# PEER query weights multiplied as fp32 without a split, nine chunks of them loaded into idle memory, and a new order of ring slots

## The reference

```python
h = rms_norm(x, norm2_g[l]) * (1 + scale2) + shift2
q = (h @ w_q).reshape(B, S, 8, 2, 128)              # w_q: 1024 x 2048
sk = einsum('bshpd,hpnd->bshpn', q, sub_keys)       # 8 heads, 2 halves, 128 keys
top_s, top_i = top_k(sk, 16)                        # per half
best_s, best_pos = top_k(all 256 sums of a head, 16)
gates = softmax(best_s)
act = gelu(einsum('tkd,td->tk', u[idx], h))         # 128 experts per token
y = einsum('tk,tkd->td', gates * act, v[idx])
x = x + gate2 * y
```

## Time and profile before

| | |
|---|---|
| time, median of 3 runs | 1796.01 us (1795.46 to 1796.23) |
| the profiled execution | 1796.63 us |
| its span | 1794.8 us |
| busy share PE / DVE / ACT / POOL | 83% / 74% / 32% / 28% |
| bytes moved | 663.24 MB, mean 370 GB/s |

### The profile page before, as it was taken

The page is one execution under the profiler, slowest core; times in us unless marked ns, Lnnn a source line. Parts: engine busy times, 40 slices in busy tenths (PEclk is TensorE's granted clock), DMA queues, the critical chain, the costliest instruction groups (busy, mean ns, idle before and its releaser), DMA issues.

```text
span 1794.8 us, 17891 instructions
## 1 busy us (share of the span) xinstructions
PE 1485.2 (83%) x6040; PEld 886.1 (49%) x6040; DVE 1330.4 (74%) x3039; ACT 577.5 (32%) x1285; POOL 510.6 (28%) x556
## 2 busy tenths in 40 slices
PE   3999999877778787777799999997777778887787
PEld 2999896333233333333378998853333333333333
DVE  7898898776776777675579886986777676777554
ACT  3565542221222222221245664331222222221222
POOL 0000014433334343334200000243333333433430
PEclk8999999989989999999999999999898988989999
DMA  9877879999999999999967754999999999999995
GB/s 382 275 263 261 293 300 400 421 421 421 422 421 422 421 421 421 422 421 421 421 222 261 255 194 131 370 421 421 421 422 421 421 422 421 421 422 421 422 421 221
DMA packets 102619, 663.24 MB, mean 370 GB/s; under 512 B 11776, under 2 KB 11904, under 8 KB 31488
## 3 DMA queue, kind: packets, MB, share of 16 engines
q0 software_dynamic: 79488, 578.85, 78.6%
q1 hardware_dynamic: 23040, 83.26, 13.2%
HBM read 661.01 MB, written 1.05 MB: 369 GB/s over the span
## 4 chain that ended last, share of the span: by engine, by line
DMA 45%; PE 36%; DVE 13%; ACT 2%; issue 2%; SPq 1%; POOL 0%; DVEq 0%; ACTq 0%
DMA big<-pairs,big 24%; DMA late<-pairs,big 21%; PE yac L707 15%; PE acc L448 10%; PE pg L448 5%; DVE big L1259 2%; DVE wsp L427 1%; DVE late L1259 1%; DVE big L1079 1%; PE acc L601 1%; DVE big L1145 1%; PE acc L574 1%; DVE big L1144 1%; ACT big L895 1%; DMA big<-ada 1%
## 5 line engine op out<-in xcount | busy, mean ns | idle before, releaser
L707 PE MATMUL yac<-big 128*128 128x512 f32 x1216 | 605.2, 646 | 190.0 <-ACT big L895 190.0
L707 PEld LDWEIGHTS yac<-big 128*128 128x128 f32 x1216 | 240.7, 204 | 533.8 <-issue 273.9
L1464 POOL DMA_INDIRECT big<-pairs,big x304 | 289.6, 953 | 599.1 <-PE yac L707 492.3
L707 PE MATMUL yac<-late,big 128*128 128x512 f32 x832 | 401.0, 624 | 58.0 <-ACT big L895 58.0
L707 PEld LDWEIGHTS yac<-late,big 128*128 128x128 f32 x832 | 164.0, 201 | 285.0 <-issue 198.1
L1464 POOL DMA_INDIRECT late<-pairs,big x208 | 199.4, 959 | 275.9 <-PE yac L707 248.1
L1259 DVE CUSTOM_DVE_ANT_0 big<-big,acc 128x1024 f32<-128x1024 f32 x148 | 179.9, 1220 | 113.4 <-DMA big<-pairs,big 113.1
L448 PE MATMUL acc<-hs,wsp 128*128 128x256 f32 x2016 | 260.1, 287 | 3.6 <-DVE wsp L427 3.6
L886 ACT ACTIVATE big<-big 128x4 f32<-128x4 f32 (+1 forms) x138 | 28.3, 205 | 709.6 <-DVE big L1259 709.6
L448 PEld LDWEIGHTS acc<-hs,wsp 128*128 128x128 f32 x2016 | 247.3, 192 | 10.7 <-issue 9.9
L1259 DVE CUSTOM_DVE_ANT_0 big<-big,pg 128x1024 f32<-128x1024 f32 x156 | 187.4, 1219 | 78.0 <-DMA big<-pairs,big 77.5
(11 more groups left out here) (137 smaller groups left out, 1018.6 us busy)
## 6 DMA issues: line engine op xcount, KB each, us to landing
raw<-stream SPq DMA_DIRECT2D x132, 512.0 KB, 4.5
big<-ada_pairs POOLq DMA_DIRECT2D x40, 1024.0 KB, 7.2
big<-ada SPq DMA_DIRECT2D x16, 512.0 KB, 13.7
big<-pairs,big POOLq DMA_INDIRECT x304, 21.5
late<-pairs,big POOLq DMA_INDIRECT x208, 22.0
big<-subkeys SPq DMA_DIRECT2D x2, 1024.0 KB, 13.6
x<-xT SPq DMA_DIRECT2D x1, 1024.0 KB, 10.1
con<-consts SPq DMA_DIRECT2D x1, 706.0 KB, 4.6
```

What stands on the lines that cost most here:

```text
L707: mm = pe.matmul(yac[:, 2 * t + w, :], diag(n), row(L, n)[:, D + w * 512:D + (w + 1) * 512], start=(n % (SLOTS // TT) == 0), stop=(n % (SL ...
L1464: g.indirect_dma_start(row(L, n), None, pairs, bass.IndirectOffsetOnAxis(ap=col(Q_IDX + n).bitcast(U32), axis=0)).then_inc(row_in[SLOT_OF[ ...
```

## The change

1. The query weights are no longer split. PE multiplies the raw fp32 chunk with the fp32 source in `big` (B_H): one fp32 matmul of 256 columns per 128 rows in place of three fp32r ones. The 16 `act_high` and 16 `dve_low` of these chunks go, the low part of the source goes too. `h2_by_tokens` has 8 transposes in place of 16 matmuls.
2. Chunks 4 to 12 are *parked*: nine loads go straight to idle pieces of `big` (in places 0, 1, 6, 7 of the ring and half of 5), issued by SP once the last output product is done. Chunks 0 to 3 and 13 to 15 still go through the raw buffers, which come free when their product is done (`wq_done`).
3. Chunks 0 and 1 are first made for tokens 0 to 127 alone (`query_first`), so that head 0's scores of that half come out early; their other half follows.
4. The `late` places are free at once. The picks' places begin with `FIRST`: 8 to 13, 2, 3, 0, 1, 6, 7, twice. Places 0, 1, 6, 7 wait for the parked chunks in them: for chunks 5, 7, 9 and 11 to be multiplied. Places 4 and 5 hold the source and wait for the second `h2_by_tokens`.
5. DVE runs heads 0 and 1 of the search without a break, then groups 0 to 3 of the dots with head 2 between them. Four groups of `add_pick`, not two, stand among the chunks, behind 7, 9, 11 and 13.

```diff
+LOWS = 3
-TOPK_WQ = ((1, 0, 0), (1, 0, 1), (1, 0, 2), (2, 0, 3), (4, 1, 0), (4, 1, 1), (5, 1, 2), (6, 1, 3),
-           (9, 2, 0), (9, 2, 1), (11, 2, 2), (11, 2, 3))
-DOTS_WQ = (8, 10)
-GATES_WQ = (9, 11)
-GELU_WQ = (9, 11)
-DIAG_WQ = (10, 12)
-PICKS_WQ = (11, 13)
-EXP_WQ = 6
+H2TOK_WQ = 3
+EXP_WQ = 4
+GELU_WQ = (6, 8, 10, 12)
+PICKS_WQ = (7, 9, 11, 13)
-CYCLE = [0, 1, 2, 3, 8, 9, 4, 5, 6, 7, 10, 11, 12, 13]
+FIRST = [8, 9, 10, 11, 12, 13, 2, 3, 0, 1, 6, 7]
+CYCLE = FIRST[:2] + [4, 5] + FIRST[2:]
+BRIDGE = CYCLE[:12] + FIRST[:2] + CYCLE[12:]
+LAST_CYCLE = BRIDGE[2:]
+SLOT_OF = (FIRST * 2 + CYCLE * 8 + BRIDGE + LAST_CYCLE * 8)[:SLOTS]
+PARK_AT = (0, CH, ROW, ROW + CH, 6 * ROW, 6 * ROW + CH, 7 * ROW, 7 * ROW + CH, 6 * ROW - CH)
+M_PARK = M_WQ + 4
...
+                    if n == M_PARK:
+                        chunk_used(sp, L, M_OUT + N_OUT - 1)
+                        for j in range(PARKED):
+                            load_parked(L, j)
...
+            def query(L, c, out, t0, t1):
+                for k in range(KD):
+                    mm = pe.matmul(out, chunk_raw(L, M_WQ + c)[:, k * P:(k + 1) * P], col(B_H + k * T + t0, t1 - t0),
+                                   start=(k == 0), stop=(k == KD - 1))
+                return mm
...
+            def query_first(L):
+                pe.wait_ge(acc_free, nth(L, EVACS, E_WQ + 2))
+                for c in range(2):
+                    raw_landed(pe, L, M_WQ + c)
+                for k in range(KD):
+                    pe.wait_ge(src_hi, nth(L, 4 * KD, 3 * KD + k + 1))
+                    for c in range(2):
+                        mm = pe.matmul(acc[:, (E_WQ + c) % 2, 0:P], chunk_raw(L, M_WQ + c)[:, k * P:(k + 1) * P],
+                                       col(B_H + k * T, P), start=(k == 0), stop=(k == KD - 1))
+                mm.then_inc(q0_done, 1)
+                pe.wait_ge(q0_taken, L + 1)
+                pe.wait_ge(subkeys_in, nth(L, 16, 16))
+                for p in range(2):
+                    mm = pe.matmul(yac[:, 2, p * P:(p + 1) * P], col(B_QP + p * T, P), col(B_SUB + p * P, P),
+                                   start=True, stop=True)
+                mm.then_inc(sk0_done, 1)
+                for c in range(2):
+                    query(L, c, acc[:, (E_WQ + c) % 2, P:T], P, T).then_inc(wq_done, 1)
...
-                first_two(L, M_WQ, E_WQ, 3)
-                head_subkeys(L, 0)
+                query_first(L)
                 for c in range(2, N_WQ):
-                    by_features(L, M_WQ + c, E_WQ + c)
-                    if c >= 4 and c % 2 == 0:
+                    query_chunk(L, c)
+                    if c == 2:
+                        head_subkeys(L, 0)
+                    elif c == 3:
+                        head_subkeys(L, 1)
+                    elif c >= 6 and c % 2 == 0:
                         head_subkeys(L, c // 2 - 1)
...
-                source(L, 3, 1)
-                for c in range(N_WQ):
...
+                normalised(nth(L, 2, 2), gs[:, KD:2 * KD])
+                for n in range(len(ADA_WQ)):
+                    ada_next(L, ADA_OUT + N_OUT + n)
+                for u in range(2):
+                    scores_in(L, u)
+                    for part in range(4):
+                        topk_part(L, u, part)
+                unit_gates(L, 0)
+                for g in range(len(GELU_WQ)):
+                    pick_dots(L, g)
+                    pick_weights(L, g)
+                    if g < 2:
+                        if g == 0:
+                            scores_in(L, 2)
+                        topk_part(L, 2, 2 * g)
+                        topk_part(L, 2, 2 * g + 1)
...
                     before = USES[r].index(n) - 1
                     if before >= 0:
                         pool.wait_ge(slot_done, L * SLOTS + USES[r][before] + 1)
-                    elif RING_BIG <= r < RING_BIG + W:
-                        pool.wait_ge(chunk_done, (L + 1) * SPLITS + r - RING_BIG + 1)
-                    elif r >= RING_BIG + W:
+                    elif r >= RING_BIG:
+                        pool.wait_ge(chunk_done, (L + 1) * SPLITS + min(r - RING_BIG + 1, W))
+                    elif r in (4, 5):
                         pool.wait_ge(h2tok_done, L * TT + TT)
+                    else:
+                        inside = [j for j, at in enumerate(PARK_AT) if at // ROW == r]
+                        if inside:
+                            pool.wait_ge(wq_done, nth(L, N_WQ, M_PARK - M_WQ + inside[-1] + 1))
```

More of the change, by code:

```diff
@@ L286, in build @@
         index_done = sem("index_done")
+        parked_in = [sem(f"parked_in{j}") for j in range(PARKED)]
+        wq_done = sem("wq_done")
+        q0_done = sem("q0_done")
+        q0_taken = sem("q0_taken")
+        sk0_done = sem("sk0_done")
+        sk0_taken = sem("sk0_taken")
         row_in = [sem(f"row_in{r}") for r in range(RING)]
@@ L445, in product @@
                 if source is not None:
-                    pe.wait_ge(src_done, nth(L, 4 * KD, source * KD + k + 1))
+                    pe.wait_ge(src_done, nth(L, LOWS * KD, source * KD + k + 1))
                 for n, (a, b) in enumerate(TERMS):
@@ L461, in _, with load, load_next, load_parked @@
             sp.dma_start(cact, cB).then_inc(c_in, 16)
[L463 to L471, removed]
+            def load(L, m):
+                n = streamed(L, m)
+                sp.dma_start(raw[:, n % RAW, :], stream[nth(L, CHUNKS, m), :, :]).then_inc(landed[n % RAW], 16)
+            def load_next(L, m):
+                before = m - RAW
+                if before < M_PARK + PARKED <= m:
+                    before -= PARKED
+                if before < SPLITS:
+                    sp.wait_ge(split_done, nth(L, SPLITS, before + 1))
+                else:
+                    sp.wait_ge(wq_done, nth(L, N_WQ, before - M_WQ + 1))
+                load(L, m)
+            def load_parked(L, j):
+                sp.dma_start(col(PARK_AT[j], CH), stream[nth(L, CHUNKS, M_PARK + j), :, :]).then_inc(parked_in[j], 16)
             def load_first(k):
@@ L494, in _ @@
             for L in range(depth):
-                for n in range(RAW, SPLITS):
+                for n in range(RAW, CHUNKS):
+                    if n == M_PARK:
+                        chunk_used(sp, L, M_OUT + N_OUT - 1)
+                        for j in range(PARKED):
+                            load_parked(L, j)
+                    if parked(n):
+                        continue
                     load_next(L, n)
@@ L678, in h2_by_tokens @@
                 for k in range(KD):
[L679 to L683, removed]
+                    mm = pe.transpose(out[:, k // 4, k % 4 * P:(k % 4 + 1) * P], col(B_H + k * T + t * P, P), ident)
                 mm.then_inc(h2tok_done, 1)
             def head_subkeys(L, h):
-                if h == 0:
-                    pe.wait_ge(subkeys_in, nth(L, 16, 16))
                 pe.wait_ge(acc_free, nth(L, EVACS, E_WQ + 2 * h + 1 + 3))
@@ L694, in head_subkeys @@
                 out = yac[:, 2 + h % 2, :]
-                for t in range(TT):
+                for t in range(0 if h else 1, TT):
                     for p in range(2):
@@ L812, in modulated @@
                     act.wait_ge(xn_done, nth(L, 2 * KD, w * KD + k + 1))
-                    nc_act.activation(hs[:, 0, k * T:(k + 1) * T], col(B_H + k * T, T), ACT.Identity,
+                    out = col(B_H + k * T, T) if w else hs[:, 0, k * T:(k + 1) * T]
+                    nc_act.activation(out, col(B_H + k * T, T), ACT.Identity,
                                       bias=mod[:, 24 * w + k:24 * w + k + 1]).then_inc(src_hi, 1)
@@ L977, in _ @@
                 a.clear()
-                for c in range(N_WQ):
[L979 to L983, removed]
+                query_first_store(L)
+                for c in range(2, N_WQ):
+                    query_store(L, c)
+                    if c == 2:
                         store_subkeys(L, 0)
-                    if c >= 4 and c % 2 == 0:
+                    elif c == 3:
+                        store_subkeys(L, 1)
+                    elif c >= 6 and c % 2 == 0:
                         store_subkeys(L, c // 2 - 1)
```

122 lines of the change are left out of this document (70 added, 52 removed).

## The result

The changed kernel takes 1824.72 us (median of 4 runs, 1824.24 to 1825.77), the one before in the same session 1796.12 (1795.46 to 1796.34). The ratio is 1.0162, with a 95% interval of 1.0148 to 1.0175: 28.6 us slower, where 23 were forecast (1819 us, range 1803 to 1831). The profiled execution has a span of 1823.9 us, 29.1 more than before.

What follows compares the result with a forecast made beforehand. The prediction took the DMA stream at 421 GB/s as the bound, so time lost before each plateau counts. Layer 0 +10.9, layer 1 +9.6 and slower PE starts +2.8 made +23 us: 1819 us, range 1803 to 1831.

Steps and rivals of the forecast that it cites:

- The measure: Before each layer's DMA plateau: lost transfer time, length x (1 - rate/421), each microsecond lost being one of the end.
- Part 1, the products: PE's query products: an fp32 chunk takes 3.41 us, 0.5 more than a split one.
- Part 2, the first indices: Head 0's search in layer 0: begins at 229.0, first gather issued near 236.0, 3.8 us earlier.
- Parts 3 and 4, the order and the waits: PE's chunks and POOL's in-order waits, layer 0: pick 10 goes at 272.0 behind chunk 9, pick 11 at 286.5 behind chunk 11.
- Part 5, the ledger: DMA losses before the plateau: 29.1 us against 18.2 in layer 0, 40.2 against 30.6 in layer 1.
- The two big holes: DMA gaps ahead of picks 10 and 11: 7.7 and 12.0 us in layer 0, 10.9 and 12.0 in layer 1.
- The first row: From the output stage to the full DMA queue: 7.7 us lost in layer 0, 14.3 in layer 1.
- the second starvation: Behind the second transposes PE waits for head 1's dots; pick 30's bytes flow just when the queue runs dry, loss put at 0.
- rival C: Starvation behind the second transposes costs 3 to 6 us per layer: 1825 to 1831 us and more; chance 13%.
- the slower PE behind a stand: PE's start on group 2 of the picks after standing some 8 us: 1.4 us per layer, +2.8 in all.
- Rival A: DMA queue stays fed, no hole before picks 10, 11 and 26: 1769 us, milder form near 1777; chance 11%.
- Rival B: No change: chunk near 2.8 us or PE about 5 us per pair of chunks faster, 1793 to 1799 us; chance 6%.

Runs made afterwards that it cites:

- e4: Changed kernel with another order of places: places 6 and 7, which wait for chunks 9 and 11, come only at picks 18 and 19; 1808.79 us, ratio 1.0054.
- e10: e9 with the four groups of picks one chunk later, behind chunks 8, 10, 12 and 14; 1787.61 us, ratio 0.9946.
- e8: Changed kernel with six of the eight 128-row pieces in every query product; 1807.46 us, ratio 1.0060.
- e5: e1 plus the edit of e3 and a new order of places, with places 4 and 5 at picks 28 and 29; 1792.18 us, ratio 0.9965.
- e1: Changed kernel with nothing parked, all 16 query chunks going through the four raw buffers; 1803.35 us, ratio 1.0030.
- e2: e1, but gathers into places 0, 1, 6 and 7 still wait for chunks 5, 7, 9 and 11; 1827.92 us, ratio 1.0169.
- e7: Changed kernel with two groups of picks among the query chunks, behind 11 and 13, in place of four; 1813.97 us, ratio 1.0096.
- e11: e5 without the edit of e3, so head 1's exponential stays behind the last query copies; 1805.94 us, ratio 1.0053.
- e3: Changed kernel with the exponential of head 1's picks moved to behind ACT's copy of chunk 14; 1820.01 us, ratio 1.0124.
- e9: e5 with chunks 4 to 7 parked again in places 0 and 1, which come last in the round, at picks 10 and 11; 1791.57 us, ratio 0.9973.

## Why the prediction was right

**The measure.** Transfer time lost before the plateau, per layer, was the right currency. The eleven kernels that followed came out within 3 us of their expectations by the medians; against the kernel before of their own session e4 and e10 gained some 4 us more than expected. Each was worked out with the traces so far at hand, so they bear the account out, and not the first forecast.

**Part 1, the products.** 3.41 us forecast, 3.46 measured. That they don't cost one for one is shown by e8 (0.6 of a microsecond for each) and by e5, which has the same products and is faster than the kernel before. That they cost by way of the waits is what e8's gathers 10 and 11 suggest, 5.6 and 7.4 us earlier.

**Part 2, the first indices.** 236.0 forecast, 237.4 measured, in a run whose output stage ended 0.5 us later. The slower start was as charged (L742: 5.44 us for 32 records), with some luck: behind the same stand of 2.17 us the same products took 3.81 us in both layers of e1 and in one layer each of e2, e7 and e11.

**Parts 3 and 4, the order and the waits.** Chunks 9 and 11 released gathers at 274.3 and 289.0, forecast 272.0 and 286.5; e2 and e4 show, from both sides, that the waits and their rank in POOL's order are the cause.

**Part 5, the ledger.** The two big holes were right to 2 us. The first row was too large in layer 0 by 3.1 us, all of it in the output stage: 2.8 us were lost there, 5.7 forecast. From there to 267 it is 1.8 us for a forecast of 2.0, but not where I put it: the start of the parked loads cost 0.6 us (287 GB/s from 219.1 to 221.1), the rest came later.

**The mis-sized term** is the one put at zero: the second starvation, ahead of pick 30, which I had as rival C with "zero slack". It measured 3.1 and 3.2 us; e3 takes 4.7 of these 6.3 back, so it is shown. So a part of rival C came true, at its lowest price (3 to 6 us per layer), and the time lies where the forecast ends and rival C begins (1825). Of the 3.1 us in layer 0 about 1.0 is the longer stand (8.89 us, where 334.7 - 326.8 = 7.9 was forecast) and about 2 the slow first pick behind it: pick 30 was issued 344.27 - 340.22 = 4.05 us after PE's start, where 339.2 - 2.4 - 334.7 = 2.1 was forecast. The other is the slower PE behind a stand, 1.4 per layer in the sum, which measured 9.50 - 7.0 = 2.5 behind the first stand and 3 behind the second. The granted clock says what it is: 0.68 of full speed in the windows from 334 and from 1226, and in shorter ones 0.50, which is the lower of the two levels (1.2 GHz), from 296.85 to 300.00, at the start of the first group behind the first stand, and behind the second stand:

```profile
335.00:340.00 5.00, 0.00 (x0) 0.00 (x0) 4.86 (x16) 0.44 (x2) 0.96 (x2) 0.58 1.00 418
340.00:345.00 5.00, 4.78 (x6) 2.19 (x7) 4.97 (x13) 4.21 (x9) 0.73 (x1) 0.50 0.78 324
```

By the Trainium skill, "TensorE: Matmul & The Clock Gate", section on HAM oscillation, a burst of matmuls behind a wait for transfers starts cold; the trace agrees for the stands of 8 to 9 us, with the 0.50 above. Only the first of the two goes back to a transfer (the dot at 294.70 waited 13.80 us for pick 11's row); the second is a wait for the exponential.

In the table, forecast to measured: +6.3 ahead of pick 30, +1.7 ahead of pick 26, +2.4 ahead of picks 10 and 11, -3.4 in the first row, together +7.0, of which 5.6 show in the time. The -3.4 is luck: without it the measured time would have been some 9 us above the forecast, near the upper end of the range.

**Rival A**, the queue that stays fed, fell: 57 GB/s from 267 to 292 us, where it needed 421. **Rival B** fell with the length of the products (3.46 us, where it needed about 2.8).

## What to carry to other kernels

A queue that issues in order turns one late place into a stop for all that is behind it: give the ring's places an order by the time at which they come free, and look at what the DMAs do while the first of them is waited for. Loading weights ahead pays only if the memory that they sit in isn't needed by the stream that they make room for, and only until the next bound (here the second transposes and PE's picks, which free the ring's places); e9 shows the early gain given back within 100 us. In a kernel with a plateau of full bandwidth, count what is lost before the plateau, window by window, for both versions; here it adds up to the end within about 1 us (30.3 for 29.1).

## What the runs showed of the hardware that was not expected

Behind a stand of PE of 8 to 9 us, fp32 matmuls of 512 columns took about twice their time at first: 6.57 us for the eight records of 340.22, 3.4 to 3.6 elsewhere. Behind 3.65 us the same eight took 5.40 (e3). So the price of a stand is not the stand alone: in the changed kernel it is some 2.5 and 3 us more per layer.

Behind a short stand it isn't the same every time. PE stands 2.17 us ahead of the 32 first products in every one of the twelve traces of the changed kernel and its variants; the products took 5.3 to 5.4 us in most (e8 has only 24 of them, 4.5 us), at a granted clock of 0.69 in the changed kernel, and 3.81 us, at 1.00, in both layers of e1, layer 0 of e2 and e11 and layer 1 of e7. A difference of 1.6 us per layer between two traces can be this alone. No run shows what decides it.
